# A token factor from feature-major squares, and token parts straight from PSUM, between the last attention layer and the experts of a Trainium2 encoder kernel

## What is computed

```python
def odd_layer(x, norm1, w_in, ..., w_out, norm2, router, exp_gate, exp_up, exp_down):
    p = rms_norm(x, norm1) @ w_in
    x = x + gla_mixer(p, ...) @ w_out
    return x + moe_swiglu(rms_norm(x, norm2), router, exp_gate, exp_up, exp_down)

def rms_norm(x, g, eps=NORM_EPS):
    y = x * lax.rsqrt(jnp.mean(x * x, axis=-1, keepdims=True) + eps)
    return y * g
```

## Time and profile before

| | |
|---|---|
| median of three runs | 1643.25 us (1642.49 to 1643.83) |
| profiled execution, device time | 1644.72 us |
| span of its profile, first to last instruction | 1642.9 us |
| TensorE busy | 1569.9 us (96%) |
| VectorE busy | 1259.3 us (77%) |
| ScalarE busy | 1055.2 us (64%) |
| mean granted TensorE clock | 0.988 |
| the chain that ended last: TensorE's share of the span | 61% |

### The profile page before, as it was taken

The page is one execution under the profiler, slowest core; times in us unless marked ns, Lnnn a source line. Parts: engine busy times, 40 slices in busy tenths (PEclk is TensorE's granted clock), DMA queues, the critical chain, the costliest instruction groups (busy, mean ns, idle before and its releaser), DMA issues.

```text
span 1642.9 us, 29979 instructions
## 1 busy us (share of the span) xinstructions
PE 1569.9 (96%) x11044; PEld 1234.9 (75%) x11044; DVE 1259.3 (77%) x1524; ACT 1055.2 (64%) x1425; POOL 0.2 (0%) x4
## 2 busy tenths in 40 slices
PE   7987888999999899999999999999999999999997
PEld 6866787999999878777777777777776777777774
DVE  6855436656555875789889899889889989889886
ACT  5663344444445435777777777777777777778774
POOL 0000000000000000000000000000000000000000
PEclk9988999999999999999999999999999999999999
DMA  8002004444544313699999999999999999999993
GB/s 338 11 1 117 4 4 155 181 171 184 191 156 154 116 42 118 244 379 359 365 371 369 355 369 368 361 365 371 361 368 368 353 372 373 353 368 363 368 369 119
DMA packets 100923, 425.42 MB, mean 259 GB/s; under 512 B 8160, under 2 KB 8160, under 8 KB 95344
## 3 DMA queue, kind: packets, MB, share of 16 engines
q1 hardware_dynamic: 100848, 424.38, 68.8%
HBM read 423.30 MB, written 1.05 MB: 258 GB/s over the span
## 4 chain that ended last, share of the span: by engine, by line
PE 61%; DVE 1%; ACT 0%; issue 0%; DVEq 0%
PE bank L158 19%; PE bank L156 19%; PE bank L157 19%; PE bank L1866 1%; PE bank L1886 1%; PE bank L1816 1%; DVE w_low L153 0%; PE bank L2141 0%; PE bank L1839 0%; ACT xn L2168 0%; DVE x_tok_low L2032 0%; ACT scratch L2170 0%; DVE xn L2119 0%; DVE bank L2107 0%; PE bank L1805 0%
## 5 line engine op out<-in xcount | busy, mean ns | idle before, releaser
L153 DVE TENSOR_TENSOR w_low<-ring,w_high 128x1024 fp32r<-128x1024 f32 x801 | 932.1, 1217 | 45.6 <-ACT w_high L150 45.5
L150 ACT ACTIVATE w_high<-ring 128x1024 fp32r<-128x1024 f32 x801 | 799.9, 1049 | 73.7 <-PE bank L158 53.9
L156 PE MATMUL bank<-w_high,slots_high 128*96 128x512 f32 x448 | 179.6, 401 | 0.0
L156 PE MATMUL bank<-w_high,more_slots_high 128*96 128x512 f32 x448 | 179.6, 401 | 0.0
L156 PE MATMUL bank<-w_high,turned_high 128*96 128x512 f32 x448 | 175.0, 391 | 2.3 <-DVE turned_low L153 2.1
L158 PE MATMUL bank<-w_high,more_slots_low 128*96 128x512 f32 x448 | 176.8, 395 | 0.0
L158 PE MATMUL bank<-w_high,slots_low 128*96 128x512 f32 x448 | 176.8, 395 | 0.0
L158 PE MATMUL bank<-w_high,turned_low 128*96 128x512 f32 x448 | 176.6, 394 | 0.0
L157 PE MATMUL bank<-w_low,turned_high 128*96 128x512 f32 x448 | 175.9, 393 | 0.0
L157 PE MATMUL bank<-w_low,slots_high 128*96 128x512 f32 x448 | 175.4, 391 | 0.0
L157 PE MATMUL bank<-w_low,more_slots_high 128*96 128x512 f32 x448 | 175.3, 391 | 0.0
(11 more groups left out here) (346 smaller groups left out, 2424.2 us busy)
## 6 DMA issues: line engine op xcount, KB each, us to landing
ring<-in_w_moe SPq DMA_DIRECT2D x224, 1024.0 KB, 6.5
ring<-in_w_moe SPq DMA_DIRECT2D x224, 512.0 KB, 6.1
ring<-in_w_ffn SPq DMA_DIRECT2D x22, 1536.0 KB, 6.6
ring<-in_w_in SPq DMA_DIRECT2D x15, 1536.0 KB, 6.8
ring<-in_w_out SPq DMA_DIRECT2D x6, 1536.0 KB, 7.5
scratch<-in_x SPq DMA_DIRECT2D x2, 512.0 KB, 4.2
out_y<-xn SPq DMA_DIRECT2D x4, 256.0 KB, 2.9
const<-in_const SPq DMA_DIRECT2D x1, 948.0 KB, 13.2
```

The lines of the kernel that those rows point to most:

```text
L150: return nc.scalar.activation(dst, src, ACT.Copy)
L153: return nc.vector.tensor_tensor(dst, src, high.bitcast(f32), sub)
L156: nc.tensor.matmul(out, left[0], right[0], start=start, stop=False, **flags)
```

## The change

The squares of the residual are taken on ScalarE from the feature-major `xT` as its pairs become ready, and 16 small TensorE products (128 x 128 squares as the stationary side, one column of ones as the moving one) sum them over the features, giving one column for each block of tokens. The factor is computed from these sums. The turned residual stays in PSUM, in banks 0, 1, 4 and 5, and both the high and the low part of the tokens are read from there, in four parts of 128 x 512. The copy of the residual to `x_res` is put between evacuations of the gather (after the 6th, 9th, 11th and 13th), since it is needed only at the end; but it must be done before TensorE writes banks 4 and 0 with expert products, for which there is a new semaphore `res_copied`. The five dummies are gone, and half of the transposes come after the token sums.

```diff
--- before.py
+++ after.py
@@ -1717,7 +1717,7 @@
         (logits_ready, gap_ready, gap_exp, chosen_ready, ranks1_ready, routed, res_turned) = (
             sem(n) for n in ("logits_ready", "gap_ready", "gap_exp", "chosen_ready", "ranks1_ready", "routed",
                              "res_turned"))
-        router_gain, logits_t, token_sq, token_rstd = area(misc + 192, KT * E), area(misc + 256, S), area(7680, D), area(misc + 512, 2, TT)
+        router_gain, logits_t, token_sq, token_rstd = area(misc + 192, KT * E), area(misc + 256, S), area(0, KT, S), area(misc + 512, TT)
         (router_ready, logits_t_ready, logits_t_copied, token_rstd_ready) = (
             sem(n) for n in ("router_ready", "logits_t_ready", "logits_t_copied", "token_rstd_ready"))
 
@@ -1740,7 +1740,8 @@
                              "silu_e_ready", "hidden_e_ready", "turned_e", "turned_high", "turned_ready", "down_e_done", "y_high",
                              "y_split_ready", "scattered", "x_added"))
         TURNS = FET // RING - 1
-        stored = sem("stored")
+        TURN_BANK = [0, 1, 4, 5]
+        stored, token_sq_ready, token_sum_ready, res_copied = (sem(n) for n in ("stored", "token_sq_ready", "token_sum_ready", "res_copied"))
 
         SUM_BANK = [2, 3, 6, 7]
         GATHER_BANK = [2, 3, 7, 6]
@@ -1819,16 +1820,18 @@
                     return last
 
                 first_four = range(4) if half == 0 else ()
-                if first_four:
-                    pe.wait_ge(x_tok_high, TT)
+                if first_four and p == 0:
+                    pe.wait_ge(x_tok_high, 2)
                 for k in first_four:
                     gather_part(k, 0)
-                if first_four:
-                    pe.wait_ge(x_tok_ready, TT)
+                if first_four and p == 0:
+                    pe.wait_ge(x_tok_ready, 2)
                 for k in range(KT):
                     i = KT * half + k
                     if i >= 4:
                         pe.wait_ge(gathered_copied, N_GATHERS * p + i - 3)
+                        if i == 4 and p == 0:
+                            pe.wait_ge(x_tok_ready, 4)
                         gather_part(k, 0)
                     gather_part(k, 1).then_inc(gathered, 1)
 
@@ -1917,6 +1920,8 @@
             for half in range(2):
                 gather(half)
             pe.wait_ge(slots_ready, 2 * e0 + 2)
+            if p == 0:
+                pe.wait_ge(res_copied, 4)
             unit(0, 0, 0, 0)
             for n in range(2):
                 turn_places(n)
@@ -2000,6 +2005,10 @@
                                      ps[GATHER_BANK[i % 4]][:, 0:HALF * CAP].rearrange("p (e c) -> p e c", e=HALF), ACT.Copy,
                                      scale=par("o_norm2", k))\
                     .then_inc(gathered_copied, 1)
+                if p == 0 and i in (5, 8, 10, 12):
+                    n = (5, 8, 10, 12).index(i)
+                    act.wait_ge(x_tok_ready, n + 1)
+                    nc.scalar.activation(x_res[:, n % 2, (n // 2) * 512:(n // 2 + 1) * 512], ps[TURN_BANK[n]][:, :], ACT.Copy).then_inc(res_copied, 1)
                 if i == KT - 1:
                     act.wait_ge(gathered_copied, N_GATHERS * p + KT)
                     for n in range(2):
@@ -2019,6 +2028,13 @@
             expert(E - 2, 0)
             expert(E - 1, 1, last=True)
 
+        def x_tok_low_part(dve, n):
+
+            t, columns = n % 2, slice(n // 2 * 512, n // 2 * 512 + 512)
+            dve.wait_ge(x_tok_high, n + 1)
+            nc.vector.scalar_tensor_tensor(x_tok_split[1][:, t, columns], ps[TURN_BANK[n]][:, :], token_rstd[:, t:t + 1],
+                                           x_tok_split[0][:, t, columns].bitcast(f32), mul, sub).then_inc(x_tok_ready, 1)
+
         def place_slots(dve, p):
 
             dve_then(dve, nc.vector.tensor_scalar(rank_p, rank, float(CAP * p - 1), None, sub))
@@ -2027,10 +2043,8 @@
             for half in range(2):
                 experts, n = slice(HALF * half, HALF * (half + 1)), HALF
                 if half and p == 0:
-                    for t in range(TT):
-                        dve.wait_ge(x_tok_high, t + 1)
-                        nc.vector.scalar_tensor_tensor(x_tok_split[1][:, t], x_res[:, t], token_rstd[:, 1, t:t + 1],
-                                                       x_tok_split[0][:, t].bitcast(f32), mul, sub).then_inc(x_tok_ready, 1)
+                    for m in range(1, 4):
+                        x_tok_low_part(dve, m)
                 for t in range(TT):
                     nc.vector.tensor_tensor(place[:, t, experts], cst("slots").unsqueeze(1).to_broadcast([P, n, CAP]),
                                             rank_p[:, t, experts].unsqueeze(2).to_broadcast([P, n, CAP]), ALU.is_equal).then_inc(placed, 1)
@@ -2111,6 +2125,7 @@
             expert(E - 2, 0)
             expert(E - 1, 1, last=True)
             dve.wait_ge(scattered, p + 1)
+            dve.wait_ge(res_copied, 4)
             if p:
                 dve.wait_ge(stored, 64 * p)
             for r in range(4):
@@ -2129,30 +2144,36 @@
             def _(pe):
                 project_out(pe, G_OUT1, T_OUT1, 4)
                 def turn_res(n):
-                    pe.wait_ge(out_added, 8 + 2 * (n // 2) + 2)
                     for k in range(4 * (n // 2), 4 * (n // 2) + 4):
-                        last = nc.tensor.transpose(ps[n][:, (k % 4) * P:(k % 4 + 1) * P], xT[:, k, (n % 2) * P:(n % 2 + 1) * P], ident)
+                        last = nc.tensor.transpose(ps[TURN_BANK[n]][:, (k % 4) * P:(k % 4 + 1) * P], xT[:, k, (n % 2) * P:(n % 2 + 1) * P], ident)
                     last.then_inc(res_turned, 1)
 
                 pe.wait_ge(router_ready, 1)
                 for k in range(KT):
                     if k % 2 == 0:
                         pe.wait_ge(out_added, 8 + k // 2 + 1)
-                    last = nc.tensor.matmul(ps[4][0:E, 0:S], router_gain[:, k * E:(k + 1) * E], xT[:, k], start=(k == 0), stop=(k == KT - 1))
+                    last = nc.tensor.matmul(ps[7][0:E, 0:S], router_gain[:, k * E:(k + 1) * E], xT[:, k], start=(k == 0), stop=(k == KT - 1))
                 last.then_inc(logits_t_ready, 1)
-                for n in range(4):
-                    turn_res(n)
+                turn_res(0)
+                turn_res(1)
                 pe.wait_ge(logits_t_copied, 1)
                 for t in range(TT):
                     last = nc.tensor.transpose(ps[6][:, t * E:(t + 1) * E], logits_t[0:E, t * P:(t + 1) * P], ident[0:E, 0:E])
                 last.then_inc(logits_ready, 1)
-                keep_running(pe, 5, 7)
+                pe.wait_ge(token_sq_ready, 4)
+                for t in range(TT):
+                    for k in range(KT):
+                        last = nc.tensor.matmul(ps[3][:, t:t + 1], token_sq[:, k, t * P:(t + 1) * P], cst("ones")[:, 0:1],
+                                                start=(k == 0), stop=(k == KT - 1))
+                last.then_inc(token_sum_ready, 1)
+                turn_res(2)
+                turn_res(3)
                 pe.wait_ge(chosen_ready, 1)
-                nc.tensor.matmul(ps[5][:, 0:E], cst("before"), chosen[:, 0], start=True, stop=True)
-                nc.tensor.matmul(ps[5][:, E:2 * E], cst("ones"), chosen[:, 0], start=True, stop=False)
-                nc.tensor.matmul(ps[5][:, E:2 * E], cst("before"), chosen[:, 1], start=False, stop=True)
-                nc.tensor.matmul(ps[5][:, 2 * E:3 * E], cst("ones"), chosen[:, 0], start=True, stop=False)
-                nc.tensor.matmul(ps[5][:, 2 * E:3 * E], cst("ones"), chosen[:, 1], start=False, stop=True).then_inc(ranks1_ready, 1)
+                nc.tensor.matmul(ps[2][:, 0:E], cst("before"), chosen[:, 0], start=True, stop=True)
+                nc.tensor.matmul(ps[2][:, E:2 * E], cst("ones"), chosen[:, 0], start=True, stop=False)
+                nc.tensor.matmul(ps[2][:, E:2 * E], cst("before"), chosen[:, 1], start=False, stop=True)
+                nc.tensor.matmul(ps[2][:, 2 * E:3 * E], cst("ones"), chosen[:, 0], start=True, stop=False)
+                nc.tensor.matmul(ps[2][:, 2 * E:3 * E], cst("ones"), chosen[:, 1], start=False, stop=True).then_inc(ranks1_ready, 1)
                 keep_running(pe, 4, 7)
                 all_passes(pe, moe_products)
 
@@ -2160,19 +2181,26 @@
             def _(act):
                 split_high(act, G_OUT1 + 1)
                 split_high(act, G_OUT1 + 2, T_OUT1 + 3)
+                def token_square(j):
+                    act.wait_ge(out_added, 8 + j + 1)
+                    nc.scalar.activation(token_sq[:, 2 * j:2 * j + 2], xT[:, 2 * j:2 * j + 2], ACT.Square).then_inc(token_sq_ready, 1)
+
+                token_square(0)
+                token_square(1)
                 act.wait_ge(tile_done, T_OUT1 + 2 * GROUP)
-                for n in range(2):
-                    front_high_part(act, G_MOE, n, 0)
+                front_high_part(act, G_MOE, 0, 0)
+                token_square(2)
```

(26 more changed lines are left out.)

## The result

The changed kernel took 1648.36 us (median of 14 runs, 1645.69 to 1649.32), the kernel before 1643.92 us beside it (median of 14, 1641.64 to 1646.77). The ratio is 1.0024, with a 95% interval of 1.0016 to 1.0032: slower by 4.4 us, outside my range of 1642.3 to 1646.2. It is close to what I had given for the case on the slower side, 1647.4 at 6%.

A forecast was written before the change was run, and what follows sets the result against it. TensorE's own work was taken to bound the expert stage, so the first expert product's start decides: -0.3 earlier factor, 0 late ranks, +1.0 copies, +0.7 us together, giving 1644.0 us, with an 8-in-10 range of 1642.3 to 1646.2.

The forecast's parts named there:

- the case on the slower side: Clock stays low for two stretches around the rank products: 0.7 + 2 x 1.7 = 4.1 us, 1647.4 us; 6%.
- What bounds the kernel: Expert stage, last 980 us: TensorE's own work, so a shift of the first expert product moves the end equally.
- Rank products: TensorE ahead of the gathers: token products at 0.115 us per record, rank products starting 0.9 us late at 643.4.
- VectorE's chain: Ranks and places on VectorE: all moves by 0.9 us, first two `place` done at 646.9.
- the wait that goes: TensorE's 0.67 us wait for `x_tok_low` disappears and pays for late ranks; low gather products at 648.4, as before.
- Token factor: ScalarE ahead of the gather evacuations: free at 649.0, 0.27 us earlier; fifth gather starts at 649.8 instead of 649.96.
- Four copies: ScalarE copies among gather evacuations, 0.55 us each, delay the first expert product to 659.1; +1.0 us in the sum.
- if its pace of 0.54 was set by waits and not by its work: Cheaper-copies rival: ScalarE catches up during the gathers, copies cost nothing, about -1.2 us, 1642.1 us; cheaper case 14%.
- The clock: Rival before the gathers: TensorE's clock falls once, 3.4 us at 1.2 GHz, +1.7 us, 1645.7 us; 25%.
- the case for that: Low clock for two stretches if turning and rank products do not bring it back; 4.1 us, 1647.4 us; 6%.

The follow-up runs named there:

- 32 columns: Changed kernel with 32 columns of ones instead of 1 as moving side of the token products; 1650.46 us in one execution.
- wide products: Changed kernel with 128 columns of ones instead of 1 as moving side of the 16 token products; 1644.82 us, ratio 0.9997.
- reordered kernel: Against wide products: ranks before second transposes, low parts after first places, next weights' high parts in ScalarE's idle time, copies on VectorE; 1642.70 us, ratio 0.9991.

## Why the prediction was wrong, point by point

*What bounds the kernel.* Right: the expert stage is 984.5 us before (1642.9 - 658.36) and 985.2 after, from first expert product to the end, it stayed between these in 13 of the 14 profiles (986.2 with 32 columns, where the clock was low for 6.8 us behind the slots' weights), and what was lost ahead of it was lost at the end.

*Rank products, VectorE's chain, the wait that goes.* Right, where the clock holds. With wide products the sums took 0.115 us per record, as taken; the ranks started 5.79 us behind the first transpose against 4.89 before, the 0.90 that I had worked out; and the low gather products were reached after 10.64 us against 10.80, 0.16 earlier where I had 0.04.

*Token factor.* Right in kind: the fifth gather starts after 12.03 us against 12.32, 0.29 earlier where I had 0.16. The two hand-overs that I had put in without a row decided nothing: the logarithm came 0.21 us behind the sums where I had 0.15, and the first evacuation started when the table load was over (647.35), not when its bank was full.

*Four copies.* The mechanism is there (a wait of TensorE at the end of the gathers), the term is mis-sized: +1.0 forecast (0.9 against TensorE alone, 659.1 - 658.2), 0.20 measured. I had read ScalarE's pace, 0.54, from eight evacuations. The first six of the kernel before show its own:

```profile
649.27 2.94 ACT L1999 ACTIVATE scratch<-bank,param 128x384 f32<-128x384 f32 x6
```

(2.94 - 0.58)/5 = 0.47, where 0.58 is the last record's own length. The other two took (4.32 - 2.94)/2 = 0.69 each, the 0.70 in which TensorE fills a bank: they waited for it. With 0.47 for an evacuation and 0.48 for a copy the path is 649.0 + 13 x 0.47 + 0.88 + 4 x 0.48 = 657.9 where I had 659.1, and TensorE alone needs 658.2, so by this sum the copies would cost nothing and the 0.20 is left over. The condition stood among my rivals ("if its pace of 0.54 was set by waits and not by its work"), and a shorter window would have settled it. Without the fall of the clock, as the kernel with wide products has it, the change as a whole is worth -0.09 us, not +0.7.

*The clock.* This is the step that failed: "The change opens no long wait, which speaks against this". It took the absence of idle time as evidence for a full clock, since the one fall that I had shown stood behind a wait. Here TensorE was busy 26 of 26 us and the clock fell all the same. The price failed with it: one stretch of 3.4 us at a loss of half, 1.7, when 10.2 us, three times that, came in a row. The order that I had read from the program, transposes and eight-column ranks behind the sums, is the one that went with the long fall in every profile; the case for that had 6%. That its 1647.4 lies near the measured 1648.36 is luck: it is made of +0.7 for the change without a fall, measured as -0.09, and of two stretches at 1.7, where one of three times the length cost 4.17. The loss by the rows: the end of the sums comes after 5.75 us instead of 4.91 (+0.84), the eight transposes take 1.74 instead of 0.88 (+0.86), the rank products 2.00 instead of 1.03 (+0.97), from there to the gathers 3.19 instead of 2.32 (+0.87: the dummies, at 0.40 us a record, last longer than VectorE needs for the places), and the first eight gathers 2.26 instead of 1.50 (+0.76): 4.30, of which 0.13 is made up later, and 4.17 is what the wide products gave back.
The Trainium skill (TensorE: Matmul & The Clock Gate, part 1, What's actually happening) has the gate follow how busy the array has been. The records' busy time does not stand in for that here: it is 26.00 of 26 us at 0.80, and at 1.00 it is 25.65 of 26 us with wide products and 26.00 in the reordered kernel. But records overlap (with wide products two rank records last 0.37 us together, and the next two start 0.22 us after their start), so their sum does not say how much the array does, and the page's rule is not refuted by it. The rule of part 4 on transposes, which I had cited, is not needed for the fall: all 16 of them are also in the kernel with wide products, at 1.00. In the changed kernel they did not bring the slow clock back, which agrees with it, but neither did the eight dummy records for 3.2 us behind them, so this is no test of the rule.

## What to carry to other kernels

Small products with one moving column are not neutral on TensorE: a run of them can bring its clock down while the engine shows as busy, and where transposes and more small products followed in line, it stayed down. Where a record takes as long with one moving column as with many, widen the moving side (64 and 128 columns held the clock here, 32 did not): it cost 0.1 us at most and gave 4.2 us back, twice what dummies among them did. Price a slow clock by what it meets, not by its length, and read an engine's pace only from instructions whose input was already there.

## What the hardware showed that I had not expected

- 3.4 us at 1.2 GHz cost 0 us in one kernel (20.68 against 20.72). Against the kernel with wide products, 3.4 us cost 0.98 in another order of the work, and 10.2 us cost 4.17.
- 32 records of 128 x 128 weights take the same time, to 0.1 us in all, with 1, 64 and 128 moving columns (0.112 to 0.115 us each) at full clock.
- Whether the clock falls behind the 32 one-column records of the slots' weights changes from one execution to the next of the same kernel: 3.4 us in one profile of the changed kernel, none in the other.
- ScalarE makes a 128 x 384 evacuation every 0.47 us and a 128 x 512 copy out of PSUM every 0.48 us, though single records read 0.58 and 0.62.
